# Laying the expert weights of a mixture-of-experts block four rows to a partition, with one pass for narrow token blocks

## The reference

```python
logits = (xt @ w_router + b_router).astype(jnp.float32)
top_v, top_i = lax.top_k(logits, TOP_K)                  # 4 of 32
gates = jax.nn.softmax(top_v, axis=-1).astype(h.dtype)
...
gu = xblk @ w_gate_up[e] + b_gate_up[e]                  # 1024 x 2048
x_glu = jnp.minimum(gu[:, :D_EXPERT], SWIGLU_LIMIT)
x_lin = jnp.clip(gu[:, D_EXPERT:], -SWIGLU_LIMIT, SWIGLU_LIMIT)
act = x_glu * jax.nn.sigmoid(SWIGLU_ALPHA * x_glu) * (x_lin + 1)
return act @ w_down[e] + b_down[e]                       # 1024 x 1024
```

## Time and profile before

| | us |
|---|---|
| median of 3 runs | 1183.38 |
| range of the runs | 1183.0 to 1183.73 |
| span of the profiled execution | 1182.6 |
| PE busy in it | 1021.1 (86%) |
| DVE busy | 294.9 (25%) |
| ACT busy | 179.9 (15%) |
| moved by DMA | 464.91 MB, mean 393 GB/s |

### The profile page before, as it was taken

The page is one execution under the profiler, slowest core; times in us unless marked ns, Lnnn a source line. Parts: engine busy times, 40 slices in busy tenths (PEclk is TensorE's granted clock), DMA queues, the critical chain, the costliest instruction groups (busy, mean ns, idle before and its releaser), DMA issues.

```text
span 1182.6 us, 21683 instructions
## 1 busy us (share of the span) xinstructions
PE 1021.1 (86%) x8300; PEld 506.5 (43%) x8301; DVE 294.9 (25%) x813; ACT 179.9 (15%) x453; POOL 31.7 (3%) x54
## 2 busy tenths in 40 slices
PE   4999999977886999899979997999799979696966
PEld 4847887433342343334333433343335333333333
DVE  4636664241120121112111211121111211111112
ACT  3213340221110111101110111011111111010002
POOL 1001002110000000000000000000000000000000
PEclk9999999978898999999989998999899989898989
DMA  9899925989999979999999999999999999999996
GB/s 351 324 383 378 338 109 225 423 344 413 424 425 425 422 299 425 425 425 425 425 426 426 426 426 425 426 420 426 426 426 407 426 427 426 425 425 426 426 425 252
DMA packets 61485, 464.91 MB, mean 393 GB/s; under 512 B 5901, under 2 KB 10061, under 8 KB 28569
## 3 DMA queue, kind: packets, MB, share of 16 engines
q1 hardware_dynamic: 60736, 462.47, 94.8%
q0 software_dynamic: 336, 1.07, 0.3%
q10 hardware_dynamic: 392, 1.09, 0.2%
HBM read 462.50 MB, written 2.11 MB: 393 GB/s over the span
## 4 chain that ended last, share of the span: by engine, by line
PE 66%; DMA 21%; DVE 5%; issue 4%; ACT 2%; SPq 1%; POOL 0%; DVEq 0%; ACTq 0%
PE pp L1539 24%; DMA arena<-in_w_down_dram 18%; PE pp L1570 14%; PE pp L1325 5%; PE pp L1503 4%; PE pp L1247 2%; PE pp L1338 2%; PE pp L1257 2%; PE po L1400 2%; PE po L1484 2%; PE pp L1512 2%; DMA gain<-gain_dram 2%; DMA arena<-in_w_ada_dram 1%; PE pp L1518 1%; ACT work L720 1%
## 5 line engine op out<-in xcount | busy, mean ns | idle before, releaser
L1539 PE MATMUL pp<-arena,work 128*32 128x256 f32 (+1 forms) x3840 | 373.9, 445 | 20.1 <-ACT work L720 20.1
L1570 PE MATMUL pp<-arena,work 128*32 128x256 f32 (+1 forms) x1920 | 203.6, 466 | 86.8 <-issue 86.8
L1539 PEld LDWEIGHTS pp<-arena,work 128*32 128x32 f32 (+1 forms) x3840 | 166.7, 117 | 211.1 <-issue 125.9
L1570 PEld LDWEIGHTS pp<-arena,work 128*32 128x32 f32 (+1 forms) x1920 | 83.3, 124 | 188.0 <-issue 169.9
L1091 DVE TENSOR_SCALAR work<-pp 128x128 f32<-128x128 f32 (+1 forms) x74 | 25.0, 338 | 402.6 <-PE pp L1539 402.6
L723 ACT ACTIVATE work<-work 128x128 f32<-128x128 f32 (+1 forms) x74 | 25.9, 350 | 403.0 <-DVE work L1091 403.0
L1085 DVE COPY work<-pp 128x256 f32<-128x256 f32 (+1 forms) x37 | 19.5, 526 | 255.4 <-PE pp L1503 255.4
L1503 PE MATMUL pp<-h_sb,work 128*32 128x256 f32 (+1 forms) x480 | 68.1, 467 | 16.1 <-issue 11.2
L1484 PE MATMUL po<-work 64*128 64x512 f32 x304 | 75.5, 615 | 1.2 <-ACT work L739 1.2
L1325 PE MATMUL pp<-arena 128*128 128x256 f32 x256 | 57.1, 382 | 0.0
L804 DVE SCALAR_TENSOR_TENSOR h_sb<-arena,small,h_sb 128x1024 f32<-128x1024 f32 x38 | 49.5, 1303 | 11.1 <-DMA arena<-in_w_ada_dram 9.9
(11 more groups left out here) (224 smaller groups left out, 621.4 us busy)
## 6 DMA issues: line engine op xcount, KB each, us to landing
arena<-in_w_gate_up_dram SPq DMA_DIRECT2D x128, 2048.0 KB, 29.5
arena<-in_w_down_dram SPq DMA_DIRECT2D x32, 2048.0 KB, 34.4
arena<-in_w_down_dram SPq DMA_DIRECT2D x64, 1024.0 KB, 21.6
arena<-in_w_ada_dram SPq DMA_DIRECT2D x11, 2048.0 KB, 14.4
arena<-in_w_in_dram SPq DMA_DIRECT2D x4, 2048.0 KB, 19.6
arena<-in_w_gate_dram SPq DMA_DIRECT2D x4, 2048.0 KB, 13.3
arena<-in_w_out_dram SPq DMA_DIRECT2D x2, 2048.0 KB, 10.1
arena<-in_w_ada_dram SPq DMA_DIRECT2D x2, 1024.0 KB, 13.1
```

What stands on the lines that cost most here:

```text
L1539: mm = t_.matmul(pp[j * m:(j + 1) * m, UP[hh], 0:w].rearrange("p (s f) -> p s f", s=2), hgT[:, at:at + m], gu_w[slot][:, k, :, r * PAIR:(r ...
L1570: mm = t_.matmul(pp[j * m:(j + 1) * m, UP[0], 0:w], actT[:, at:at + m], wd[:, j * w:(j + 1) * w], start=(n == 0), stop=(n == KD - 1))
```

## The change

The down weights are laid four adjacent rows to a partition. The lower half then is one run of 16 KB for each partition; the upper half is still loaded in two parts, each 8 KB of a run of 16 KB. The activations must come out in the same order, so the columns of gate and up are taken in pairs: half `h` of a group of 512 columns has columns 4n + 2h and 4n + 2h + 1. A narrow block has four column groups and thereby room for all 1024 gate and 1024 up columns in one bank (256 of each for each group), so it now does one pass of 512 columns where it did two of 256; the elementwise work, the signals and the copy of the activations become one step (a signal counts two). A wide block keeps its two halves, over other columns. The bias now has two rows of 512 columns in place of four of 256, and shares its place with gain2; its first loads therefore wait until gain2 has been written to HBM and stand further back in SP's order. At the end gain2 is read into a free weight page.

```diff
-BR = 256
+BR = 512
 NBR = F // BR
...
+        gain2_back = page(2, D)
...
-        gain2 = sb("gain2", [P, D])
+        gain2_bias = sb("gain2_bias", [P, D + BR])
+        gain2 = gain2_bias[:, 0:D]
...
-        bgu = sb("bgu", [96 + NBR, 2, BR])
+        bgu = gain2_bias[0:96 + NBR, D - BR:D + BR].rearrange("p (s f) -> p s f", s=2)
...
-        dn_v = w_down[0].rearrange("e (g p r) n -> e p g (r n)", p=P, r=2)
+        dn_v = w_down[0].rearrange("e (g p r) n -> e p g (r n)", p=P, r=4)
...
+        def parts_of(m, halves):
+            return (tuple(enumerate(halves)), 1) if m == TB else (((0, halves[1]),), 2)
...
             def load_dlo(slot, e):
-                sp.dma_start(dlo_w[slot].rearrange("p (g r) d -> p g (r d)", r=2),
-                             dn_v[e, :, 0:2, :]).then_inc(s_dlo[slot], 16)
+                sp.dma_start(dlo_w[slot].rearrange("p k d -> p (k d)"),
+                             dn_v[e, :, 0, :]).then_inc(s_dlo[slot], 16)
...
             def load_dhi(e, r):
                 sp.dma_start(dhi_w[:, 2 * r:2 * r + 2, :].rearrange("p k d -> p (k d)"),
-                             dn_v[e, :, 2 + r, :]).then_inc(s_dhi[r], 16)
-
-            load_bgu(0, 0)
-            load_bgu(1, 1)
+                             dn_v[e, :, 1, 2 * r * D:2 * (r + 1) * D]).then_inc(s_dhi[r], 16)
...
             for slot, i in ((0, 1), (0, 2), (1, 3)):
                 load_gu(slot, slot, i)
+            sp.wait_ge(s_gspill, 16)
+            load_bgu(0, 0)
+            load_bgu(1, 1)
             sp.wait_ge(s_merged, KD)
             load_dlo(0, 0)
...
-            sp.dma_start(gain2[:], gain2_dram[0:1, :].to_broadcast([P, D])).then_inc(s_gback, 16)
+            sp.dma_start(gain2_back, gain2_dram[0:1, :].to_broadcast([P, D])).then_inc(s_gback, 16)
...
-                    for hh in range(2):
-                        act.wait_ge(s_aT, halves[hh])
-                        a.copy(actT[:, hh * w // 2:(hh + 1) * w // 2],
-                               pp[:, (TOKS, TURN)[hh], 0:w // 2]).then_inc(s_aTev, 1)
+                    for hh, n in parts:
+                        act.wait_ge(s_aT, n)
+                        a.copy(actT[:, hh * PAIR:(hh + 1) * PAIR],
+                               pp[:, (TOKS, TURN)[hh], 0:PAIR]).then_inc(s_aTev, n_signals)
...
+                def up_of(j, hh):
+                    return pp[j * m:(j + 1) * m, UP[hh], :].rearrange("p (s n c) -> p s n c", s=2, c=2)
+
+                def pairs(cols, h):
+                    return cols.rearrange("p s (n h c) -> p s h n c", h=2, c=2)[:, :, h, :, :]
...
-                    for hh in range(2):
+                    for hh, _ in parts:
                         for j in range(tiles):
-                            r, cols = half_of(j, hh)
-                            mm = t_.matmul(pp[j * m:(j + 1) * m, UP[hh], 0:w].rearrange("p (s f) -> p s f", s=2),
-                                           hgT[:, at:at + m], gu_w[slot][:, k, :, r * PAIR:(r + 1) * PAIR][:, :, cols],
+                            g, h = columns_of(j, hh)
+                            mm = t_.matmul(up_of(j, hh), hgT[:, at:at + m],
+                                           pairs(gu_w[slot][:, k, :, g * BR:(g + 1) * BR], h),
                                            start=False, stop=(k == KD - 1), skip_group_check=True)
```

More of the change, by code:

```diff
@@ L156, in block_program @@
         nblk_i, wide_i, expert_i = tabs[:, 0, :], tabs[:, 1, :], tabs[:, 2, :]
-        bgu = sb("bgu", [96 + NBR, 2, BR])
-        bm = [bgu[32 * h:32 * h + NMOD, :, :].rearrange("p s f -> p (s f)") for h in range(2)]
+        bgu = gain2_bias[0:96 + NBR, D - BR:D + BR].rearrange("p (s f) -> p s f", s=2)
+        bm = [gain2_bias[32 * h:32 * h + NMOD, D:D + BR] for h in range(2)]
         grids = gain2[0:NEXP, 0:16 * NEXP].rearrange("p (n e) -> p n e", e=NEXP)
@@ L362, in small_loads @@
                     sp.dma_start(scale, g_pre_ffn[0:1, :].to_broadcast([P, D])).then_inc(s_gain[2], 16)
-                    sp.dma_start(gain2[:], g_post_ffn[0:1, :].to_broadcast([P, D])).then_inc(s_gain[3], 16)
+                    sp.dma_start(gain2, g_post_ffn[0:1, :].to_broadcast([P, D])).then_inc(s_gain[3], 16)
                     sp.dma_start(wr, w_router[0].rearrange("(k p) e -> p k e", p=P)).then_inc(s_wr, 16)
@@ L973, in _ @@
             dve.wait_ge(s_gain[3], 16)
-            v.tensor_tensor(gain2[:], gain2[:], flat2(mod_bank(5)), ALU.mult).then_inc(s_mod_v, 1)
+            v.tensor_tensor(gain2, gain2, flat2(mod_bank(5)), ALU.mult).then_inc(s_mod_v, 1)
             v.memset(y_sb, 0.0).then_inc(s_zero, 1)
@@ L1492, in block_of, with columns_of @@
                 q = w // P
-                def half_of(j, hh):
-                    return (2 * j + hh, slice(0, PAIR)) if w > PAIR else (j, slice(hh, PAIR, 2))
+                parts, n_signals = parts_of(m, halves)
+                def columns_of(j, hh):
+                    return (j, hh) if m == TB else (j // 2, j % 2)
+                def up_of(j, hh):
+                    return pp[j * m:(j + 1) * m, UP[hh], :].rearrange("p (s n c) -> p s n c", s=2, c=2)
+                def pairs(cols, h):
+                    return cols.rearrange("p s (n h c) -> p s h n c", h=2, c=2)[:, :, h, :, :]
                 pe.wait_ge(s_bgu[slot], landed * 2)
@@ L1508, in block_of @@
                 for j in range(tiles):
-                    for hh in range(2):
-                        rows = bias_rows_of(slot, hh)
-                        r, cols = half_of(j, hh)
-                        t_.matmul(pp[j * m:(j + 1) * m, UP[hh], 0:w].rearrange("p (s f) -> p s f", s=2),
-                                  pick[rows, r, 0:m], bgu[rows, :, cols], start=True, stop=False,
+                    for hh, _ in parts:
+                        g, h = columns_of(j, hh)
+                        rows = bias_rows_of(slot, h)
+                        t_.matmul(up_of(j, hh), pick[rows, g, 0:m], pairs(bgu[rows, :, :], h), start=True, stop=False,
                                   skip_group_check=True)
@@ L1520, in block_of, with turn_part @@
                 mm.then_inc(s_turn, 1)
-                def turn_half(hh):
-                    pe.wait_ge(s_actv, halves[hh])
-                    for i in range(q // 2):
-                        mm = t_.transpose(pp[:, (TOKS, TURN)[hh], i * P:(i + 1) * P], sig[:, hh, i:w // 2:q // 2],
-                                          ident[:])
-                    mm.then_inc(s_aT, 1)
+                def turn_part(hh, n):
+                    pe.wait_ge(s_actv, n)
+                    for i in range(2):
+                        mm = t_.transpose(pp[:, (TOKS, TURN)[hh], i * P:(i + 1) * P], sig[:, hh, i:PAIR:2], ident[:])
+                    mm.then_inc(s_aT, n_signals)
                 pe.wait_ge(s_turned, it)
@@ L1560, in block_of @@
                         pe.wait_ge(s_dhi[k // 2 - 2], dhi_landed)
-                    if n == 2:
+                    if n == 2 and m == TB:
                         pe.wait_ge(s_aTev, halves[1])
```

40 lines of the change are left out of this document (21 added, 19 removed).

## The result

The kernel after takes 1189.26 us (median of 5 runs, 1188.9 to 1190.9), the kernel before 1183.73 beside it: the medians are 5.5 us apart. The forecast was 1182.9 us with a range of 1178.0 to 1187.5; the time lies above it. The profiled execution spans 1188.6 us, 6.0 more than that of the kernel before.

A forecast was written before the change was run, and what follows sets the result against it. The prediction took the slowest DMA engine, streaming weights, to bound the kernel. Terms -2.1 (16 KB runs), +1.9 (bias) and -0.3 (narrow blocks) summed to -0.5 us; 1182.6 - 0.5 + 0.8 gave 1182.9 us, range 1178.0 to 1187.5.

The forecast's parts named there:

- What bounds the kernel: Whole loop: from about 427 us an expert costs what its weight bytes cost, 29.9 us; compute runs beside it.
- the slowest DMA engine sets the time: Weight queue: every load waits for its slowest engine, not the mean; a few engines run up to 6 us behind.
- (e): Rival, lower down load: the 16 KB run is still cut in 8 KB packets; 1184.9 us; chance 0.03.
- The bias loads: Bias loads, four rows to two: +1.9 us taken, half of the dear end; ends -2.0 and +3.9.
- a longer tail: End of the last loads: DMA share tailing off for longer than before would show the forecast wrong; no size given.
- (b): Rival, bias loads: the dear end holds, +3.9 us, sum +1.5, 1184.9 us; chance 0.07.
- the dear end: Bias loads: slowest engine goes from 4 to 8 KB an expert, 0.154 us each over 25 experts, +3.9 us.
- The 16 KB runs: Lower down half: fewer, larger packets save 0.083 us an expert over 25 experts, -2.1 us; ends -1.5 and -5.2.
- Narrow blocks: Gate and up pass -0.5 us, bias products +0.35; at most -4.6 us of TensorE hidden by the queue, -0.3 exposed.
- Wide blocks: Gate and up pass reading pairs of columns 16 bytes apart: same work, taken as costing nothing.
- (d): Rival, wide blocks: paired read loses 4%, 0.56 us each; five rounds of 0.7 plus 1.1; 1187.5 us; chance 0.13.
- theory B: From the experiments, not the prediction: two-row bias loads sit on fewer DMA engines, and every landing waits for those.

## Why the prediction was wrong

**What bounds the kernel** was read rightly. Without 0.5 of 465 MB the kernel before is 8.1 us faster, while the run with four small matmuls in a row had 1132.5 - 1039.3 = 93 us more of TensorE's busy time than the one with them in turn, and was 48 us longer for it: half of even so much lay beside the loads. The sentence that the slowest DMA engine sets the time held more strictly than the sum then used it. Three small slips change nothing: the last slice of the earlier trace rows, 252, lies under the 299; the earlier trace rows give 1.09 - 0.68 = 0.41 for the longer bias products, not 0.35; and (e) adds up to 1185.0.

**The bias loads are the step that failed.** The price was worked out rightly: 0.154 us an expert for going from 4 to 8 KB, and the pace of the run with two rows alone rose by (60.10 - 59.82) / 2 = 0.14. But only half of it was taken, "because only part of the lag need be this". The runs without bias loads show that nearly all of the lag was bias. They also show that the tail was the wrong measure of it. An expert's bias cost 0.37 us in the kernel before, where the tail of the earlier trace rows, shared out over 25 experts, had been read as 0.24; 25 x 0.37 would be 9.3 us, and the tail was 6.5. In the kernel after, where the price is 0.54, it is 5.5, and up to 7 in the second profile. So "a longer tail", the sign of (b), did not clearly come although (b)'s mechanism was at work.

The Trainium skill's rule (page "DMA: Bandwidth & Descriptors", section "Why a DMA increments its semaphore by 16 and not by 1"), that the engines of a DMA are the largest number up to 16 that divides its slowest dimension, would have given the dear end, +3.9. The order of 2, 4 and 8 rows agrees with it (0.54, 0.37, 0.20 us), and so do the small packets of a load (two, four, eight). The 2.1 engines of the tail fit two rows, but the 1.6 of the earlier trace rows don't fit four.

The dear end was near the truth. With two rows alone the last landing is 6.5 us late, and the trace splits that up: a wide pass ahead of the empty queue and the narrow pass behind it, then the same narrow pass in the kernel before.

```profile
374.95 15.65 PE L1541 MATMUL pp<-arena,work 128*64 128x512 f32 x64 [0.68 <-ACT work L722]
...
432.04 7.51 PE L1541 MATMUL pp<-arena,work 128*32 128x256 f32 x128 [0.46 <-ACT work L722]
```
```profile
429.62 7.51 PE L1539 MATMUL pp<-arena,work 128*32 128x256 f32 x128 [0.46 <-ACT work L720]
```

Behind the empty queue the run is 2.4 us late, of which 1.7 are the wide pass, at a granted clock of 0.89 in that execution (15.65 us where 13.95 stood). From there to the last landing 4.1 us are added. So the term of +1.9, with ends of -2.0 and +3.9, measured +5.7 (4.0 to 7.4) by the ratio and 4.1 by the pace of this trace: the dear end or more, and over twice what was taken. What the ratio has beyond the 4.1 was not settled.

**The 16 KB runs** were right in sign and size by themselves: -2.1 forecast, with ends of -1.5 and -5.2; -3.2 (-4.4 to -2.0) measured, and 0.10 to 0.13 us an expert by the pace where 0.083 stood. Beside the two-row bias they gave only -1.0, so the sum took twice too much for them. That the upper half's new source costs nothing holds within that. Packets of 8 KB and more fell from 61485 - 28569 = 32916 to 57003 - 28184 = 28819, by 4097 where 4096 were forecast, so (e) did not happen.

**Narrow blocks.** The bias products got 0.42 us longer (1.10 against 0.68). The pass did not get 0.5 us shorter: the forecast took half of a wide pass that reads in a row, 6.98, for a pass that reads pairs. In a row it would have been 7.07. That none of it shows in the time was right.

**Wide blocks** were the other wrong step: "I take nothing" was 0.67 us, 4.8%. The comparison of 59 against 54.5 ns an instruction that stood there pointed to it, and was put down as agreement. The prediction took from the Trainium skill (page "SBUF — State Buffer", section "Specifications (TRN2)") that two hits in each 16-byte line make the read free; the same table row says that each cross to a new line pays a penalty, and a read in pairs crosses every two columns where a read in a row crosses every four. The measurement decides: two hits in each line did not make this read free. Rival (d) had the price a block nearly right (0.56) and 1.1 us at the empty queue, where 1.5 were seen, but its five rounds of 0.7 did not come: 537.90 us against 537.93. The share of 0.68 at 901 to 903 was no sign of TensorE at its limit. By theory B, engines that have no bias run ahead of those that have, so the mean share dips while the slow ones still work. The slices of the kernel before without bias loads fit that:

```profile
GB/s 350 314 385 375 361 110 217 423 344 415 425 426 426 417 299 425 428 427 427 425 427 428 424 428 427 424 428 426 428 424 427 428 425 427 426 428 423 427 428 306
```

From the sixteenth slice to the last but one none is under 423, where 407 stood.

So (d)'s time of 1187.5 came nearest by luck, for a reason that was mostly false, and (b)'s mechanism, priced at 1184.9, was the true one. Together, by the runs: bias +5.7, longer runs -1.0 beside it, TensorE's work about +0.4 to +1.2: +5.1 to +5.9. Against (b)'s sum of +1.5 that is 1.8 more for the bias, 1.1 less from the runs, and 0.7 to 1.5 more for TensorE, which had stood at -0.3.

What the change is worth apart from its bias can be read from three pairs with the same bias: 0.9942 against 0.9932 (none), 0.9986 against 0.9972 (eight rows), 0.9964 against 0.9953 (one load). The changed kernel is 1.2 to 1.7 us slower in each, 16 KB runs and all, though no single pair separates it from nothing.

## What to carry to other kernels

In a kernel that streams weights, a small load of few rows can cost far more than its share of the bytes: the runs here fit a price set by what it puts on the busiest DMA engine, for which every large load then waits. Leave it out once and time it, then spread it over more rows or make copies on an idle engine. When the mean DMA share tails off slowly or dips under 1 beside a full queue, look for engines that lag before looking for a late issue; but don't take the length of the tail for what the lag has cost. Where a changed layout changes the step between the elements that TensorE reads, allow for a few per cent on every pass (4.8 and 5.8 here), and look whether a neighbouring pass has that step already.

## What the runs showed of the hardware

- 16 KB of bias beside 12 MiB of weights cost 0.54 us an expert in two rows, 0.37 in four, 0.20 in eight, 0.05 in eight with half the bytes.
- A bias load of two, four or eight rows brought two, four or about eight packets under 512 B besides its data.
- Moving weights read in pairs of float32 columns 16 bytes apart take 4.8% longer with 64 stationary columns (14.62 against 13.95 us) and 5.8% with 32 (7.48 against 7.07).
- 16 small bias matmuls (8 rows, 128 columns; 32 instructions) take 2.54 us when four in a row go to one column group and 1.11 us in turn over the four groups.
